# Early projections in three rounded products, and relative-bias tables on GpSimd

## The reference

```python
# first block, two layers, each:
proj = h @ w_in[layer]              # 1024 x 4100: aq ak av ag | bq bk bv bf bg | cq ck cv cg
ya = differential attention (4 heads, two 64-wide maps each) * silu(ag)
yb = forgetting attention (4 heads; bias from the cumulated log of sigmoid(bf)) * silu(bg)
yc = stick-breaking attention (4 heads) * silu(cg)
h = layernorm(alpha * h + concat(ya, yb, yc) @ w_out[layer])
# second block, one layer:
proj = rms_norm(x) @ w_in_2         # index heads, sparse attention, hgrn2, latent attention, gates
sel = top 128 keys of each query by 8 index heads
o_a = attention over sel with bias rel_bias[t5_bucket(pos_q - pos_k)]   # 32 buckets, 4 heads
o_b = hgrn2 recurrence;  o_c = latent (MLA) attention
x = x + (g_a*(o_a @ w_up_a) + g_b*(o_b @ w_up_b) + g_c*(o_c @ w_up_c)) @ w_out_2
x = x + (silu(n @ w_gate) * (n @ w_up)) @ w_down,  n = rms_norm(x);  out = rms_norm(x)
```

## Time and profile before

| | |
|---|---|
| time of three runs | 2115.22, 2115.94 and 2116.03 us, median 2115.94 |
| span of the profiled execution | 2112.8 us; no time of its own is given for it |
| mean granted TensorE clock | 0.942 of full speed |
| busy | PE 1902.5 us, DVE 1142.6, ACT 667.5, POOL 25.4 |
| moved | 135.79 MB, 64 GB/s |

### The profile page before, as it was taken

The page is one execution under the profiler, slowest core; times in us unless marked ns, Lnnn a source line. Parts: engine busy times, 40 slices in busy tenths (PEclk is TensorE's granted clock), DMA queues, the critical chain, the costliest instruction groups (busy, mean ns, idle before and its releaser), DMA issues.

```text
span 2112.8 us, 19184 instructions
## 1 busy us (share of the span) xinstructions
PE 1902.5 (90%) x6900; PEld 1142.6 (54%) x6900; DVE 1142.6 (54%) x2306; ACT 667.5 (32%) x1340; POOL 25.4 (1%) x50
## 2 busy tenths in 40 slices
PE   5999999889899998989998876868999979999997
PEld 2444444434434444445333453556777868888785
DVE  4376676731999888532862352464445444444412
ACT  1123235311132344112112232335455334434411
POOL 2000000000000000000000000000000000000000
PEclk9999999999999998999998978978999979999998
DMA  6121112021211110032302011002333313332220
GB/s 219 40 80 40 41 49 67 27 80 40 80 40 40 40 70 1 1 111 72 89 20 60 12 59 30 14 18 75 90 90 102 113 41 99 100 98 84 98 100 40
DMA packets 153006, 135.79 MB, mean 64 GB/s; under 512 B 12673, under 2 KB 126977, under 8 KB 152913
## 3 DMA queue, kind: packets, MB, share of 16 engines
q1 hardware_dynamic: 149504, 124.53, 19.4%
q0 software_dynamic: 3408, 10.04, 1.6%
HBM read 130.36 MB, written 4.19 MB: 64 GB/s over the span
## 4 chain that ended last, share of the span: by engine, by line
PE 74%; DVE 16%; ACT 6%; issue 3%; DMA 1%; SPq 0%; DVEq 0%; ACTq 0%
PE proj L1262 24%; PE proj L1242 21%; PE proj L1259 11%; DVE rel_bias L1881 3%; PE proj L1239 2%; PE attn_out L1415 2%; PE score L1435 2%; PE score L1372 2%; PE proj L1435 1%; PE attn_out L1435 1%; PE turned_probs L1401 1%; DVE E L1951 1%; PE proj L1268 1%; PE turned_probs L1435 1%; DVE index_and_shared L1874 1%
## 5 line engine op out<-in xcount | busy, mean ns | idle before, releaser
L1262 PE MATMUL proj<-hT,weights 128*128 128x512 f32 x1216 | 561.9, 614 | 20.5 <-DVE raw L2135 11.4
L1262 PEld LDWEIGHTS proj<-hT,weights 128*128 128x128 f32 x1216 | 232.1, 196 | 302.6 <-issue 278.3
L1881 DVE SCALAR_TENSOR_TENSOR rel_bias<-index_and_shared,bias_deltas,rel_bias 128x128 f32<-128x128 f32 (+3 forms) x480 | 232.7, 547 | 4.3
L1242 PE MATMUL proj<-hT_high,weights_high 128*128 128x512 f32 x544 | 218.6, 402 | 7.6 <-DVE hT_low L2160 6.0
L1242 PE MATMUL proj<-hT_high,weights_low 128*128 128x512 f32 x544 | 215.8, 397 | 0.0
L1242 PE MATMUL proj<-hT_low,weights_high 128*128 128x512 f32 x544 | 215.5, 396 | 0.0
L2151 DVE TENSOR_TENSOR weights_low<-weights,weights_high 128x1024 fp32r<-128x1024 f32 (+1 forms) x122 | 135.3, 1116 | 96.4 <-ACT weights_high L1705 96.4
L1259 PE MATMUL proj<-weights,hT 128*128 128x512 f32 (+1 forms) x384 | 151.7, 553 | 0.1
L1705 ACT ACTIVATE weights_high<-weights 128x1024 fp32r<-128x1024 f32 (+1 forms) x122 | 111.5, 961 | 74.3 <-DMA weights<-in_w_ffn_down 60.5
L1242 PEld LDWEIGHTS proj<-hT_high,weights_high 128*128 128x128 f32 x544 | 103.2, 190 | 41.5 <-issue 9.5
L1453 ACT ACTIVATE tg<-proj 128x512 f32<-128x512 f32 x66 | 39.5, 599 | 267.0 <-PE proj L1242 212.2
(11 more groups left out here) (388 smaller groups left out, 2567.3 us busy)
## 6 DMA issues: line engine op xcount, KB each, us to landing
weights<-in_w_in SPq DMA_DIRECT2D x15, 2048.0 KB, 8.5
weights<-in_w_in SPq DMA_DIRECT2D x38, 512.0 KB, 4.2
weights<-in_w_ffn_gate SPq DMA_DIRECT2D x22, 512.0 KB, 4.1
weights<-in_w_ffn_up SPq DMA_DIRECT2D x22, 512.0 KB, 5.3
weights<-in_w_ffn_down SPq DMA_DIRECT2D x11, 1024.0 KB, 4.9
weights<-in_w_in SPq DMA_DIRECT2D x9, 1024.0 KB, 5.8
weights<-in_w_out SPq DMA_DIRECT2D x4, 2048.0 KB, 10.7
weights<-in_w_out SPq DMA_DIRECT2D x4, 1024.0 KB, 5.1
```

The lines of the kernel that those rows point to most:

```text
L1242: mm = nc.tensor.matmul(ps[:, :], w_[:, k, c0:c0 + P], x_[:, k, :], start=first, stop=last)
L1262: mm = nc.tensor.matmul(ps[0:gr["M"], :], w[:, k, c0:c0 + gr["M"]], x[:, k, :], start=first, stop=last)
L1881: ins = nc.vector.scalar_tensor_tensor(o, mk, d, o, ALU.mult, ALU.add)
```

## The change

1. All projections ahead of the tail, except those of the two latents (qb, kvb), run in the three rounded products. Slabs of 128 columns (one piece, 8 chunks, 4 KB per partition) or wide ones of 512 columns (four adjoining pieces, two chunks each) lie in two rings, one for raw pieces and one for rounded ones. The low half is written over the raw piece. `place_splits` sets ACT's copy and DVE's subtraction of each piece into the list of steps.
2. `to_hT` always gives a high part (ACT) and a low part (DVE, from PSUM), and the bank is free after the low part. y is split in eight steps before w_out.
3. w_out runs half 0 for all tiles, then half 1, each of its tiles followed by `ln`. Residual and LayerNorm now work in `h_tok`, not in `z`. The last transposes of a layer come behind two av groups; the second block starts with av.
4. The `bias` steps leave the list. POOL builds the tables: tiles 0 and 1 in layer 0, tile 2 in layer 1 (each after the lambda DMAs and before the waits for the gain rows), tile 3 after layer 1's gain rows and before the spill.
5. In the tail all pieces are 4 KB in rings of 9, and w_out_2 has two halves of 512 columns instead of four quarters.

```diff
+SLOT = 4 * (KD * (P + 8))
+RAW_RING, HIGH_RING = [SLOT * i for i in range(6)], [SLOT * i for i in range(6, 10)]
+RAW_RING_2, HIGH_RING_2 = RAW_RING[0:4], [SLOT * 8, SLOT * 9]
+TAIL_RING = 9
-N_BIAS = 4 * NT * (REL_BUCKETS - 1)
+N_BIAS = 4 * NT
-BIAS_RATES = {"A": 2.1, "B": 1.0, "C": 0.75}
...
+        for ring, on in (("raw", raws), ("high", highs if split else None)):
...
+            at = state[ring]
+            if at + n > len(on):
+                at = 0
+            sl[ring] = on[at]
+            state[ring] = (at + n) % len(on)
...
     for l in range(DEPTH):
-        sv = slab("av", layer=l)
...
+        sv = slab("av", wide=True, cols=512, layer=l)
+        wide_tiles(sv, (0, 1), dst=("V", 0), layer=l)
+        turn_rows(NT - 1, **(dict(layer=l - 1) if l else {}))
+        wide_tiles(sv, (2, 3), dst=("V", 0), layer=l)
...
+        for c in range(6):
+            steps.append(("split_x", ("y", c, 1)))
+        wo = slab("wo", wide=True, cols=512, layer=l, half=0)
...
+        wide_tiles(wo, (2, 3), dst=("resid", 0), src="y", layer=l)
+        wo = slab("wo", wide=True, cols=512, layer=l, half=1)
         for t in range(NT):
+            wide_tiles(wo, (t,), dst=("resid", 1), src="y", layer=l)
             steps.append(("ln", (l, t)))
             if final_layer:
                 if t:
                     steps.append(("norm", dict(tile=t - 1, nth=t - 1)))
+                if t >= 2:
+                    turn_rows(t - 2, layer=l, norm=t - 2)
             elif t:
+                turn_rows(t - 1, layer=l)
...
+        seq = max(p["free_high"], min(p["free_raw"] + 2, slabs[p["slab"]]["first"] - 2))
...
+    s_av = slab("avw", cols=136)
+    for t in range(NT):
+        if t == 2:
+            turn_rows(NT - 1, layer=DEPTH - 1, norm=NT - 1)
+        group("T", s_av, N=136, K=KD, tile=t, dst=("av", 0))
     for c in range(4):
+        group("F", slab("iq", c0=128 * c), K=KD, dst=("qk", 4 + c), scale=1.0)
...
+            for p in pieces:
+                consumed(sp, p["free_raw"])
...
+            def bias_tile(t):
+
+                K = P * (t + 1)
+                dist, term = below[0][:, 0:K], below[1][:, 0:K]
+                link(nc.gpsimd.tensor_scalar(dist, pkb[:, 0:K], pq[:, t:t + 1], None, ALU.subtract))
+                for b in range(REL_BUCKETS - 1, 0, -1):
+                    for h in range(4):
+                        o, d = b_at(h, t), deltas[:, b, h:h + 1]
+                        if b == REL_BUCKETS - 1:
+                            link(nc.gpsimd.tensor_scalar(o, dist, float(-BUCKET_STARTS[b]), d, ALU.is_le, ALU.mult))
+                            link(nc.gpsimd.tensor_scalar(o, o, deltas[:, 0, h:h + 1], None, ALU.add))
+                            continue
+                        link(nc.gpsimd.tensor_scalar(term, dist, float(-BUCKET_STARTS[b]), d, ALU.is_le, ALU.mult))
+                        add = nc.gpsimd.tensor_tensor(o, o, term, ALU.add)
...
             for l in range(DEPTH):
...
+                if not only_block1:
+                    if l == 0:
+                        pool.wait_ge(bias_ready, 1)
+                    for t in ((0, 1), (2,))[l]:
+                        bias_tile(t)
 
                 pool.wait_ge(ln_done, NT * (l + 1))
                 pool.wait_ge(soft1_done, soft1_at[last_B[l]])
...
             if not only_block1:
+                bias_tile(NT - 1)
                 pool.wait_ge(ln_done, n_ln)
...
+                        if s_["split"]:
+                            wh, wl = slab_view(WR, gr["slab"], "high"), slab_view(WR, gr["slab"], "raw")
+                            terms = ((wh, xh[src]), (wh, xl[src]), (wl, xh[src]))
...
+                        for k in range(begin, end):
+                            arrived(s_["pieces"][k // 2 if s_["wide"] else 0])
```

More of the change, by code:

```diff
@@ L206, in group, with used @@
         return g
[L208 to L216, removed]
+    def used(i, seq):
+        slabs[i]["last"] = seq
+        if slabs[i]["first"] is None:
+            slabs[i]["first"] = seq
     stages = [("scores", 0), ("soft1", 0), ("soft2", 1), ("soft3", 2), ("trans", 3), ("pv", 4)]
-    state = dict(lo=0, n=0, fin=0, slots=list(range(W_SLOTS)), turn=0, bias=0, bias_due=0.0, squared=None, mid=None)
-    bias_steps = [(t, b) for t in range(NT) for b in range(REL_BUCKETS - 1, 0, -1)]
+    state = dict(lo=0, n=0, fin=0, rings=(RAW_RING, HIGH_RING), raw=0, high=0, after=("ln_in", NT - 1), squared=None, mid=None)
     def tick():
@@ L373, in gate @@
         def gate(c, l=l):
[L374 to L378, removed]
+            g = group("gate", slab("ag" if c < 4 else "bgcg", c0=128 * (c % 4), layer=l), K=KD, chunk=c, layer=l,
+                      first=c >= 6)
             steps.append(("gate2", g))
@@ L430, in plan @@
             steps.append(("norm", dict(tile=NT - 1, nth=NT - 1)))
-        for t in ((NT - 2, NT - 1) if final_layer else (NT - 1,)):
-            for half in range(2):
-                group("to_hT", tile=t, half=half, layer=l, **(dict(norm=t) if final_layer else {}))
+            turn_rows(NT - 2, layer=l, norm=NT - 2)
     if not only_block1:
-        second(steps, groups, slabs, items, units, state, slab, group, weave, flush)
-    annotate(steps, groups, items, units)
-    return dict(steps=steps, groups=groups, slabs=slabs, items=items, units=units)
@@ L442, in second @@
+def second(steps, groups, slabs, items, units, state, slab, used, group, turn_rows, wide_tiles, weave, flush):
     l = DEPTH
@@ new lines, in second, with values_hi, from_rest, latents_q @@
+    hold, rot = {}, {}
+    def values_hi(t):
+        if t == 0:
+            hold["hi"] = slab("hi", wide=True, cols=512)
+        group("T", hold["hi"], N=512, K=KD, tile=t, dst=("V", 512))
+    def from_rest(name, c, dst):
+        return group("F", slab(name, c0=128 * c), K=KD, dst=dst, scale=1.0)
+    def latents_q(c):
+        if c == 0:
+            state["rings"], state["raw"], state["high"] = (RAW_RING_2, HIGH_RING_2), 0, 0
+        from_rest("mq", c, ("cq", c))
+    def kpe():
+        rot["kpe"] = from_rest("mpe", 0, ("raw", 0))
@@ L645, in second @@
             steps.append(("split_x", ("act", c, 1)))
-        steps.append(("down", dict(i=i, slab=tail[28 + KF + i])))
-        split_weights(2)
+        two = [slab("down", K=1, cols=1024, at=2 * i + k) for k in range(2)]
+        for sl in two:
+            used(sl, len(groups) + i)
+        steps.append(("down", dict(i=i, slabs=two)))
     for t in range(NT):
```

601 lines of the change are left out of this document (270 added, 331 removed).

## The result

The changed kernel takes 2579.36 us (median of 4 runs, 2578.83 to 2579.82) against 2115.58 us before (4 runs): a ratio of 1.2191, 95% interval 1.2174 to 1.2209. The forecast was 2133 us, with a range from 2030 to 2215. The profiled execution has a span of 2578.0 us.

A forecast was written before the change was run, and what follows sets the result against it. PE, 90% busy and 74% of the chain of waits, was taken as the bound; last B softmax 686, row DMAs 2 and tile 3 277 gave 965, plus rest 1165: 2130 span, 2133 us median, range 2030 to 2215.

The forecast's parts named there:

- Tile 3: 277: Layer 1, behind the last B softmax: POOL's table tile 3 takes 277 us, DVE's durations plus 0.53 us per instruction.
- Last B softmax: ... 686: Layer 1: last B softmax, which releases POOL for tile 3, moves from 763 to 686 us.
- (c): Rival: POOL and DVE hold each other up, tile 3 a third longer (277 + 80), DVE's relief gone; 2233 us, chance 0.2.
- 24 of them are 5.55 us, 1.32 less ... 150 in all: Early projections: 24 rounded products replace each 6.87 us f32 group; savings 92, 16 and 42 us, 150 in all.
- (1): Weight rings: the slab behind a wide one waits about 3 us, twice a layer; 10 us in two layers.
- (2): Output projection: wo half 0 waits for the last gate group's slots, y splits queued ahead; 5 us.
- (3): Output projection: wo half 1's DMA starts after half 0's last group; its first group ends 12.6 us later, not 5.6.
- (4): Output projection: DVE's subtraction stands behind LayerNorm; PE waits 6.8 us between half-1 groups and before the next av.
- +15: Second block: splits for the last latent groups queue in DVE behind tile 3's top-k rounds, giving back 15 us.
- Net gain 40: Before 763 us: table work off DVE saves some 59 us of chain, weight splits cost 19; 20 taken.
- (a): Rival: POOL is in time, tile 3 under 162 us, so nothing waits; 2018 us, chance 0.15.
- (b): Rival: only POOL's additions are dearer, twice DVE's, compares as on DVE; tile 3 229 us, total 2085, chance 0.2.
- (d): Rival: split pieces come too late in each woven group, 1 us in 70 groups; 2200 us, chance 0.05.

The follow-up runs named there:

- f1: Changed kernel, but GpSimd builds tile 1's table in two parts around layer 0's gain and bias rows, nothing left out; 2579.23 us (1.2212).
- e7: Changed kernel with tiles 0 to 2 of the table in full on GpSimd, tile 3 with buckets 31 and 1 only; 2256.65 us.
- e3: Changed kernel with GpSimd building only buckets 31 and 1 of the table, 29 of 31 left out; 2147.81 us (1.0154).
- e8: Kernel before (f32 products) with buckets 31 and 1 of the table only, on DVE; 2091.99 us (0.9885).
- e1: Changed kernel with the table steps back on DVE at the pace of the kernel before, rounded products kept; 2215.79 us (1.0468).
- c3: Kernel before with table tiles 0 and 1 on GpSimd, tile 1 split around layer 0's gain rows, DVE's pace adjusted; 2093.93 us (0.9913).

## Why the prediction was wrong, step by step

The sum was 965 (av's eviction) + 1165 (rest). Measured: 1364 + 1214.

**The step that failed: "Tile 3: 277".** It is wrong twice. First the price: 450 us, where the bounds were 146 and 277. My upper bound added 0.53 us to DVE's durations, but a compare-and-scale at 512 columns takes 2082 ns on GpSimd against DVE's 487, 4.3 times (DVE's row is a compare alone, GpSimd's has the scale too), and the addition 1310 against 692, 1.9 times. The bound was none: no row of the trace priced arithmetic on GpSimd. Second, the start. "Last B softmax: ... 686. Row DMAs ahead of tile 3: 2" let tile 3 begin as if tiles 0 to 2 had been done. They never were added up. With my own upper price they would have been: 996 instructions x 0.53 = 528, and 480 x (0.547 + some 0.39 for a compare, from the masks' and limits' 67 us) = 450, together 978 us from 56 on, an end at 1034 and not at 965. So of the 399 us between 965 and 1364 the missing sum makes 69 and the price 330. The trace of before had the numbers for the first part, and none for the second. The right question was not how long the last tile is but when GpSimd is through with four.

**The two waits.** The prediction named both places, the av eviction and, under what would make it wrong, a stall in layer 0. Rival (c) also had tiles 0 and 1 press on layer 0's gain rows. The 95 us in layer 0 look like a loss of their own in the view of waits. Beside the second wait they are not (f1); with it gone they are (e7).

**"24 of them are 5.55 us, 1.32 less ... 150 in all."** The group's price is right: the residual additions of wo half 0 in e3 are 5.44 us apart. PE's busy time up to the tail fell by 112 us. But that stretch did not get shorter: 1412 us before, 1441 in e3. Against the saving stood costs of 35 us before 763 us, 22 in the rest of layer 1 (164 for 158 less 16) and 29 in the second block (15 + 10 + 2 + 2), 86 in all; the idle time that e3 adds is 141.

**The ring of pieces.** (1) 3 us behind a wide slab: 3.1 and 4.1 in e3, right. (2) 5 us before wo half 0: 9.2. (3) 12.6 us for half 1's first group: half 1's first residual addition starts 14.25 us after half 0's last, and its first products run at the lower clock. (4) 6.8 us behind the LayerNorm: 5.4 twice in layer 0, then 6.7 for the next av. The stage of wo in layer 0: forecast 72, measured 74.3 in e3. The mis-sized term is "the splits for the last latent groups queue in DVE behind the top-k rounds of tile 3 ... +15": there are three such waits, behind each tile's rounds, of 57 us together, and the rest behind av's eviction is 1214 us in the changed kernel for the 1165 of the sum. For layer 0's attention I had 10 to 15 us of costs; there the idle time rose by 29: e3 has seven waits of 3 to 9 us, 32 together (splits, the rotation, softmax steps), where the kernel before has one of 3.06 us.

**"Net gain 40", of which 20 taken, for DVE's relief.** Leaving nearly all table work out is worth 25 us beside f32 products (e8) and 68 beside rounded ones (e1 to e3). The 59 us on the chain were a share of a chain, not what goes when the work goes: PE was next behind it. In the changed kernel DVE's relief was smaller: e7, with GpSimd at work up to 949 us, is 109 us above e3, 95 of them its wait for the gain rows; the other 14 fit the slower DVE instructions below, but nothing else shows them to be that.

**The rivals.** (a) and (b) needed GpSimd at DVE's speed for compares; none of it was there. (c), GpSimd and DVE hold each other up, is true in kind: beside GpSimd the addition L1792 goes from 692 to 957 ns between 100 and 850 us while L1789, one of whose inputs is in PSUM, stays at 683; e3 has 692 and 685. These rows of the changed kernel, then of e3:

```profile
L1792 DVE TENSOR_TENSOR qk<-tg,raw 128x512 f32<-128x512 f32 x14 | 13.4, 957 | 0.5
...
L1789 DVE TENSOR_TENSOR tg<-proj,constants 128x512 f32<-128x512 f32 x14 | 9.6, 683 | 3.3 <-PE proj L1286 3.2
```

```profile
L1792 DVE TENSOR_TENSOR qk<-tg,raw 128x512 f32<-128x512 f32 x14 | 9.7, 692 | 0.5
```

By the Trainium skill (SBUF — State Buffer, Who interferes with whom) an instruction of DVE with two SBUF inputs contends with a GpSimd instruction that reads SBUF, and one with a single SBUF input, outside the modes in which DVE uses two ports, doesn't; these rows agree. But (c)'s price for tile 3, "a third" (80 us; a third of 277 is 92), was small beside the price itself: GpSimd's compares run at 2.00 us when nothing is beside them, against 2.08 in the mean. (d), splits late by 1 us in each of 70 groups, wasn't so; e3 has twelve waits of PE on split weights, 106 us together.

**The bounds.** The range ended at 2215, "the upper half of (c)". It was made of prices around 277 and contained no case in which GpSimd's total was the bound.

**Better than both.** c3, tiles 0 and 1 on GpSimd and f32 products, takes 2094 us, 0.9% under the kernel before, where e8, which builds hardly any table, is 1.2% under it. There GpSimd ends at 494 us, and both places where it was late have time to spare.

## What to carry to other kernels

When work moves to an idle engine, add up all that this engine gets, from its first instruction to each deadline, before asking what the last piece costs; and treat a price that no row shows as open upwards, or measure it alone. A busy engine at 90% gives back only as much as its next rival lets it: 112 us less TensorE work returned nothing in e3, where waits on DVE's and ACT's steps grew by more than that. Of two waits on the same busy engine's queue only the last counts, until it is removed.

## What was not expected of the hardware

- On GpSimd a compare-and-scale with one tensor input is dearer than an addition with two: 2082 against 1310 ns at 512 columns, 839 against 546 at 128. The Trainium skill (GPSIMD Engine Reference, Performance versus the Vector engine, and Engine selection) has 1.96 times for the addition, here 1.89, and calls one-input work roughly line-rate; the rows have 4.3 times DVE's compare for this one, and the measurement decides. An addition of a scalar alone on GpSimd (L1182, 512 columns) takes 1.57 us in three of its four records, against 2.00 for the compare-and-scale when nothing is beside it, so the second operation is not the main part.
- GpSimd's subtractions of 1024 columns, 2.52 us each and 13% of the span, doubled a DVE addition of two SBUF operands (692 to 1337 ns).
